# A two-layer decoder trunk on one core: the attention stage in another order, with compression in four additions and o split straight from its sums

## What is computed

```python
def compress_blocks(tok, pos, w1, w2):          # 15 blocks of 32 tokens, 4 groups
    blocks = blocks + pos[:, None, :]
    return jax.nn.gelu(flat @ w1) @ w2
...
qg = h @ w_qg                                    # q, and 3 gates for each of 16 heads
s_c = q . k_cmp;  p_c = masked_softmax(s_c);  o_c = p_c . v_cmp
s_s = q . k_slc;  p_s = masked_softmax(s_s);  o_s = p_s . v_slc
s_w = q . k_win;  p_w = masked_softmax(s_w);  o_w = p_w . v_win
o = g0 * o_c + g1 * o_s + g2 * o_w
return o @ w_o
```

## Time and profile before

| | |
|---|---|
| median of 3 runs | 877.27 us (876.54 to 877.97) |
| the profiled execution | 878.77 us, span 876.9 us |
| PE busy | 814.1 us (93%), 7626 instructions |
| DVE busy | 663.0 us (76%), 734 instructions |
| ACT busy | 424.1 us (48%) |
| POOL busy | 134.6 us (15%) |
| mean granted PE clock | 0.977 of 2.4 GHz |

### The profile page before, as it was taken

How to read it: one execution, slowest core, us unless ns; L and a number is a source line. 1 busy time by engine, 2 the same in 40 slices (tenths; PEclk the granted TensorE clock), 3 DMA queues, 4 the chain that set the end, 5 groups by cost and what they waited for, 6 DMA issues and landing times.

```text
span 876.9 us, 18026 instructions
## 1 busy us (share of the span) xinstructions
PE 814.1 (93%) x7626; PEld 705.2 (80%) x7626; DVE 663.0 (76%) x734; ACT 424.1 (48%) x610; POOL 134.6 (15%) x208
## 2 busy tenths in 40 slices
PE   2899999999899899999999899998888899999997
PEld 2699798788777599999997798965566899999975
DVE  5878988999876799999996665769854687555552
ACT  3366724565463744444444645148647454444441
POOL 8700004634623100000000222001110000000000
PEclk9899999999999999999999999969999999999999
DMA  9934254234340789999992687550005377555641
GB/s 349 341 105 161 85 168 151 103 100 146 123 148 28 286 312 371 379 377 375 377 351 67 214 262 212 169 221 1 1 2 191 112 279 237 191 191 192 192 144 49
DMA packets 71840, 170.20 MB, mean 194 GB/s; under 512 B 5433, under 2 KB 6737, under 8 KB 71761
## 3 DMA queue, kind: packets, MB, share of 16 engines
q1 hardware_dynamic: 68784, 160.75, 52.6%
q0 software_dynamic: 2416, 7.15, 3.0%
q10 hardware_dynamic: 560, 1.14, 0.4%
HBM read 166.42 MB, written 1.05 MB: 191 GB/s over the span
## 4 chain that ended last, share of the span: by engine, by line
PE 59%; DVE 30%; ACT 5%; issue 3%; DMA 3%; POOL 1%; SPq 0%; DVEq 0%; ACTq 0%; POOLq 0%
DVE wlo L1123 9%; DVE acc L1509 6%; PE ps L1896 5%; PE ps L1900 5%; PE ps L1898 5%; PE ps L1885 5%; PE ps L1887 5%; PE ps L1888 5%; PE ps L1791 2%; PE ps L1793 2%; PE ps L1794 2%; PE ps L2003 2%; ACT whi L662 2%; DMA raw<-in_ada_w_dram 2%; PE ps L1767 2%
## 5 line engine op out<-in xcount | busy, mean ns | idle before, releaser
L1123 DVE TENSOR_TENSOR wlo<-raw,whi 128x2048 fp32r<-128x2048 f32 (+1 forms) x98 | 217.2, 2216 | 59.2 <-ACT whi L662 57.0
L662 ACT ACTIVATE whi<-raw 128x2048 fp32r<-128x2048 f32 (+1 forms) x98 | 179.5, 1842 | 148.1 <-DMA raw<-in_mlp_down_dram 94.7
L1885 PE MATMUL ps<-ghi,whi 128*128 128x256 f32 x576 | 164.0, 285 | 7.9 <-ACT ghi L938 4.2
L1887 PE MATMUL ps<-glo,whi 128*128 128x256 f32 x576 | 163.7, 284 | 0.0
L1888 PE MATMUL ps<-ghi,wlo 128*128 128x256 f32 x576 | 163.7, 284 | 0.0
L1885 PEld LDWEIGHTS ps<-ghi,whi 128*128 128x128 f32 x576 | 111.2, 193 | 11.2 <-issue 7.5
L1887 PEld LDWEIGHTS ps<-glo,whi 128*128 128x128 f32 x576 | 111.2, 193 | 0.5
L1888 PEld LDWEIGHTS ps<-ghi,wlo 128*128 128x128 f32 x576 | 111.3, 193 | 0.0
L1896 PE MATMUL ps<-whi,hidhi 128*128 128x512 f32 x256 | 100.9, 394 | 2.2 <-DVE wlo L1123 2.0
L1898 PE MATMUL ps<-whi,hidlo 128*128 128x512 f32 x256 | 99.8, 390 | 0.0
L1900 PE MATMUL ps<-wlo,hidhi 128*128 128x512 f32 x256 | 99.6, 389 | 0.0
(11 more groups left out here) (380 smaller groups left out, 1618.9 us busy)
## 6 DMA issues: line engine op xcount, KB each, us to landing
raw<-in_mlp_up_dram SPq DMA_DIRECT2D x32, 1024.0 KB, 5.8
raw<-in_mlp_down_dram SPq DMA_DIRECT2D x32, 1024.0 KB, 5.2
raw<-in_ada_w_dram SPq DMA_DIRECT2D x24, 1024.0 KB, 5.6
late<-in_ada_w_dram SPq DMA_DIRECT2D x24, 1024.0 KB, 9.1
late<-in_kv_ada_w_dram SPq DMA_DIRECT2D x8, 1024.0 KB, 8.9
raw<-in_kv_w_dram SPq DMA_DIRECT2D x6, 1024.0 KB, 5.7
raw<-in_rw_k_dram SPq DMA_DIRECT2D x4, 1024.0 KB, 9.1
raw<-in_rw_r_dram SPq DMA_DIRECT2D x4, 1024.0 KB, 5.1
```

Source lines behind the costliest of these rows:

```text
L662: ins = sc.activation(whi[i][:, ks, :], raw[i][:, :].rearrange("p (k n) -> p k n", k=4)[:, ks, :], ACT.Copy)
L1123: ins = dv.tensor_tensor(wlo[i][:, ks, :], raw[i][:, :].rearrange("p (k n) -> p k n", k=4)[:, ks, :], whi[i][:, ks, :].bitcast(F32), ALU.s ...
L1885: mm(out_, whi[b][:, k, cols], hi[:, k0 + k, :], start=(first and k == 0 and m % 2 == 0), stop=False, skip_group_check=True)
L1887: mm(out_, whi[b][:, k, cols], lo[:, k0 + k, :], start=False, stop=False, skip_group_check=True)
```

## The change

Lines of the changed kernel are some 5 to 20 away from those before.

- DVE's 32 `xcmp` additions are 4, each over 8 positions at once (480 columns), with the position values as a second tensor. They stand before the low part of `q0 + 1`, and the compression is PE's first step, ahead of q.
- q is written as four single steps (`query(i)`), with the gate products, turning and scores of the first units in between.
- The compressed branch is done for 8 heads at a time: `cmp_scores(h)`, `cmp_shifted(h)`, `cmp_exps(h)`, `cmp_probs(h)`, `cmp_turn(h)`, `cmp_turned(h)`. Each product of its scores repeats its 30 columns up to four times; the next one writes over the repeats.
- The maxima come negated from the reduction; the separate negation is gone.
- DVE multiplies the probabilities of all units; POOL of none.
- `oT` and its copies are gone: after `outputs(u)` ACT makes the high part of the unit's o from bank 7, and DVE the low part from bank 7 and the high part. `outputs(u)` waits for the low part of unit u - 1. The second half of the projection waits for all 16.
- The orders of PE, ACT and DVE over the stage are other ones.

```diff
-                    for p in range(8):
-                        a = 8 * h + p
-                        ins = dv.tensor_scalar(xcmp[:, i, a, 0:60].rearrange("q (g n) -> q g n", n=NCMP), src[:, p],
-                                               pt2[:, pos + a:pos + a + 1], None, ALU.add)
+                        ins = dv.tensor_tensor(
+                            xcmp[:, i, 8 * h:8 * h + 8, 0:60].rearrange("q a (g n) -> q a g n", n=NCMP), src,
+                            pt2[:, at_:at_ + 8].unsqueeze(2).unsqueeze(3).to_broadcast([P, 8, G, NCMP]), ALU.add)
...
-                st.do(dv.tensor_reduce(mx[:, u, :].rearrange("p (e b) -> p e b", e=2), src, axis=AX.X, op=ALU.max))
-                st.tell(dv.tensor_scalar(nm[:, u, :], mx[:, u, :], -1.0, None, ALU.mult), T["nm"])
+                st.tell(dv.tensor_reduce(nm[:, u, :].rearrange("p (e b) -> p e b", e=2), src, axis=AX.X, op=ALU.max, negate=True),
+                        T["nm"])
...
-                if tb == 0:
-                    st.tell(factors, T["cf"])
-                else:
...
+                keys = P * (tb + 1)
+                own = prob[u % 2][:, :, :, 0:keys].rearrange("p e b k -> p (e b) k")
+                st.tell(dv.tensor_tensor(own, own, cf[:, u, :].unsqueeze(2).to_broadcast([P, 4, keys]), ALU.mult), T["pr"])
...
+            def o_high(u):
+                act.wait_ge(n_o_ps, u + 1)
+                sc.activation(ohi[:, j, P * tb:P * tb + P], ps[:, 7, 0:P], ACT.Copy).then_inc(n_zhi, 1)
...
+            def o_low(u):
+                v.wait_ge(n_zhi, NCH + u + 1)
+                st.tell(dv.tensor_tensor(olo[:, j, cols], ps[:, 7, 0:P], ohi[:, j, cols].bitcast(F32), ALU.subtract), T["zlo"])
...
+            def cmp_scores(h):
+                pe.wait_ge(n_c, 1)
+                pe.wait_ge(n_gates, 1)
+                pe.wait_ge(n_qT, h + 1)
                 for tb in range(TB):
+                    for j in range(4 * h, 4 * h + 4):
+                        c0 = 240 * h + 2 * NCMP * (4 * tb + j - 4 * h)
+                        times = min(4, (512 - c0) // (2 * NCMP))
+                        ins = mm(ps[:, 7, c0:c0 + 2 * NCMP * times], qT[:, j, P * tb:P * tb + P],
+                                 kcmp[:, j // 2, :, 0:NCMP].unsqueeze(1).to_broadcast([P, times, 2, NCMP]), start=True, stop=True)
...
             def outputs(u):
-                pe.wait_ge(n_pcT, 1)
+                pe.wait_ge(n_pcT, 1 if j < 4 else 2)
                 if u:
-                    pe.wait_ge(n_o, u)
+                    pe.wait_ge(n_zlo, NCH + u)
+                else:
+                    pe.wait_ge(n_scx, 2)
```

More of the change, by code:

```diff
@@ L329, in hybrid_kernel @@
         n_sc_ps, n_scx, n_sce, n_pc = (sem(n) for n in ("cmp_scores", "cmp_shifted", "cmp_exp", "cmp_probs"))
[L330 to L332 removed]
+        n_pr = sem("probs_scaled")
+        n_s_ps, n_nm, n_e, n_pT_ps, n_pT, n_pcT, n_o_ps = (sem(n) for n in (
+            "scores", "score_max", "exps", "probs_turned", "probs_copied", "cmp_probs_copied", "o_psum"))
         H_AT = {1: 2, 2: 6, 3: 8, 4: 12}
@@ new lines, in cmp_blocks @@
+            def cmp_blocks():
+                v.wait_ge(n_stk, 16 * 8)
+                for i, pos in enumerate((POSK, POSV)):
+                    for h in range(2):
+                        src = stk[:, i, :, :].rearrange("q g (n s) -> q s g n", s=16)[:, 0:16:2, :, h:h + NCMP]
+                        at_ = pos + 8 * h
+                        ins = dv.tensor_tensor(
+                            xcmp[:, i, 8 * h:8 * h + 8, 0:60].rearrange("q a (g n) -> q a g n", n=NCMP), src,
+                            pt2[:, at_:at_ + 8].unsqueeze(2).unsqueeze(3).to_broadcast([P, 8, G, NCMP]), ALU.add)
+                        st.tell(ins, T["xcmp"]) if i and h else st.do(ins)
@@ new lines, in gates_copied, with inner_copied @@
+            def gates_copied():
+                v.wait_ge(n_gt_ps, 1)
+                for b in range(TB):
+                    ins = dv.tensor_copy(gates[:, b, :, :].rearrange("p h i -> p (h i)"), ps[:, 7, P * b:P * b + 48])
+                    st.tell(ins, T["gates"]) if b else st.do(ins)
+            def inner_copied():
+                v.wait_ge(n_hc_ps, 1)
+                st.do(dv.tensor_copy(both(hc), ps[0:60, 2, 0:2 * P]))
+                st.do(dv.tensor_tensor(both(hx), both(hc), both(hc), ALU.mult))
+                st.do(dv.tensor_scalar(both(hx), both(hx), 0.044715, 1.0, ALU.mult, ALU.add))
+                st.tell(dv.tensor_tensor(both(hx), both(hx), both(hc), ALU.mult), T["hx"])
@@ L2311, in _, with gate_products, query @@
-            ins.then_inc(n_hc_ps, 1)
-            q_half(1)
+            def gate_products():
+                pe.wait_ge(n_wg, 16)
+                for k in range(KC):
+                    ins = mm(ps[0:48, 7, 0:S], wg[:, k, :], hfull[:, k, :], start=(k == 0), stop=(k == KC - 1))
+                ins.then_inc(n_g_ps, 1)
+            def query(i):
+                n, kh = i // 2, i % 2
+                if kh == 0:
+                    if n:
+                        pe.wait_ge(n_kv, 2)
+                        pe.wait_ge(n_vt, 2)
+                    else:
+                        pe.wait_ge(n_kc, 1)
+                parts_ready(q0 + i)
+                features(q0 + i, 0, [ps[:, 4 * n + m // 2, (m % 2) * S:(m % 2) * S + S] for m in range(4)],
+                         qhi, qlo, 4 * kh, kh == 0).then_inc(s_ws, 1)
@@ new lines, in gates_turn, with compress_inner @@
+            def gates_turn():
+                pe.wait_ge(n_gF, 1)
+                for b in range(TB):
+                    ins = tr(ps[:, 7, P * b:P * b + 48], gateF[:, P * b:P * b + P], ident[0:48, 0:48])
+                ins.then_inc(n_gt_ps, 1)
+            def compress_inner():
+                pe.wait_ge(n_xcmp, 1)
+                pe.wait_ge(n_w1, 16 * 5)
+                pe.wait_ge(n_kv, 1)
+                pe.wait_ge(n_vt, 1)
+                for i in range(2):
+                    for p in range(16):
+                        ins = mm(ps[0:60, 2, P * i:P * i + P], xcmp[:, i, p, 0:60], w1[i][:, p, :], start=(p == 0),
+                                 stop=(p == 15))
+                ins.then_inc(n_hc_ps, 1)
```

237 lines of the change are left out of this document (90 added, 147 removed).

## The result

| | before | changed |
|---|---|---|
| median of 4 runs | 876.90 us (874.63 to 877.97) | 868.44 us (866.71 to 869.46) |
| profiled execution / its span | 878.77 / 876.9 us | 867.99 / 866.2 us |
| mean granted clock of PE | 0.977 | 0.987 |
| last product of keys and values to first of the output projection | 537.75 to 649.72 = 112.0 us | 539.77 to 638.50 = 98.7 us |

The ratio is 0.9905 [0.9879, 0.9931]: 8.5 us faster, forecast 866.3. The last line of the table is the stage that the diff touches. It is 13.2 us shorter, the span 10.7. The rest is outside the diff: the profiled execution reaches the stage 2.0 us later than the one before did, through code that is the same, and behind it 0.5 is lost. Over the fourteen profiled executions of this document the stage starts between 537.4 and 540.5 us, so 2.0 is scatter between executions.

A forecast was written before the change was run, and what follows sets the result against it. No engine full in the loop: PE, DVE and ACT wait in turn; the opening has waits and a half-speed PE clock. 14.0 - 0.4 - 0.6 - 2.0 = 11.0 us off 878.8 gives 867.8, less 1.5 is 866.3; range 863.2 to 871.5 (84%).

The forecast's parts named there:

- The walk: Hand layout of every unit through the three engines' written orders, with each wait kept: output projection 14.0 us earlier.
- Front, 10.6 us: PE's stretch from the key/value projections to scores(4): scores(4) starts at 583.5 instead of 594.15, 10.6 us earlier.
- xcmp at 0.69 each: DVE's four additions before the compression: 0.69 us each, 2.8 in all, where 32 took 9.9 with gaps.
- the test that the prediction set: Prediction counts as wrong if PE waits over 1 us for xcmp.
- Loop, 52.2 us: Loop over the attention units, from scores(4) to the output projection: 52.2 us instead of 55.6.
- Hand-overs, 2.0 us off: Some 25 hand-overs between engines on the path, at 0.05 to 0.1 us each, cost 2.0 us.
- Last low parts, 0.4; wo pieces, 0.6: Before the output projection: two last low weight parts lose 0.4 us; first wo piece may land 0.6 after ACT wants it.
- 1.5 us from profiled to median: Median of the runs shown taken as 1.5 us below the profiled execution, turning 867.8 into 866.3.
- 6.5 + 1.5 for the clock: PE at half clock in the kernel before: 6.5 us more from 578 to 591, some 1.5 from 629 to 632.
- ACT as the loop's bound: Rival: ACT gets 3.6 us more in the loop and bounds it; gain 6.0, total 871.3 us; chance 12%.
- A clock that falls again in the stage: Rival: PE's clock falls for as long as from 578 to 591, costing 5 us, total 871.3; chance 8%.
- The slower rival, bank 7 with two readers: Rival: outputs wait for ACT and DVE to read bank 7, 1.7 us per unit, total 892 us; chance 4%.

The follow-up runs named there:

- the run with the source without a step: Changed kernel with the 4 xcmp additions reading 480 neighbouring columns of another tile instead of every sixteenth column: 864.89 us, ratio 0.9843.
- the control: The changed kernel run again with no edit: 866.46 us, ratio 0.9862 to the kernel before; stage 98.7 us.
- the three groups: Three groups of runs, each on a chip of its own; the kernel before had medians of 877.99, 879.31 and 878.68 us.
- order of the front (a mixture, see above): Changed kernel with the old order of gate products, q, compression and first scores, including a 3.40 us wait neither kernel has: 874.70 us, ratio 0.9956.
- low parts behind the loop: Changed kernel with the low part of the output projection's third weight piece made inside the loop again: 869.08 us, ratio 0.9903.
- the kernel with the pause filled: Kernel before, with two unused products between scores(0) and the compressed values, where PE had waited 1.9 us: 876.60 us, ratio 0.9976.

## Why the prediction was right, and where it was not

The sum stood at 867.8 for a profiled execution and the one taken was 867.99. That is nearer than its terms were. The walk had 14.0 us and 3.0 of losses were taken off it, of which only 0.24 can be seen. The stage gave 13.2, and 2.0 of late arrival and 0.5 behind it, which were in no term, filled the place of the 3.0. The mechanism was right; that the total came out to 0.2 is luck.

- **Front, 10.6 us.** Measured 9.98 within the stage. Cover, order and clock came as laid out: compressed values under q's pieces, no wait for hcTv, clock 1.00 in all of 560 to 585, halves of 1.94 and 1.89. The compressed turn, behind the queries' last piece, stood at 581.45; the walk's 578.7 is 581.9 with the 2.0 of late arrival and the 1.2 that xcmp made.
- **xcmp at 0.69 each.** This step failed, by the test that the prediction set: PE waited 1.59. The row taken for it, the reduction of 480 elements, reads without a step. The four took 4.04 in place of 2.8, 1.01 each with their gaps, and PE started 1.2 later than laid out (541.36, against 538.1 and 2.0 of late arrival); the run with the source without a step shows that the step in the source is the whole difference. The Trainium skill (VectorE: DVE Perf Modes, Mode 2×_2P) spoke of the second tensor as the cost. The trace agrees with it in that two fp32 tensors don't get two elements a cycle: from 512 to 1024 elements the scaling, with two fp32 operands, grows by 532 ns, 1.04 ns an element, which is one element a cycle at the 0.96 GHz of that page. The 328 ns of the step come on top of that.
- **Loop, 52.2 us.** Measured 52.3. From scores(4) on to (6), (8), (10), (12) and (14) the walk had 7.6, 7.6, 8.7, 5.4 and 8.9 us; measured 7.8, 7.8, 8.3, 5.5 and 8.6. So each step came out within 0.5, and the loop's near sum doesn't rest on large errors that cancel. outputs(5) and (13) did wait for the low part of o, by 0.50 and 0.96 (forecast 0.95 and 0.7). A wait of 1.25 at turn(4) for DVE's scaling lies where the prediction shows no details. ACT's small high parts took 282 ns, not 370, so ACT got 2.2 us more and not 3.6.
- **Hand-overs, 2.0 us off.** They cost nothing that can be seen: the walk had its loop to 0.1. The 2.0 was taken off without a row of its own.
- **Last low parts, 0.4; wo pieces, 0.6.** 0.24 of wait was seen for the low part, and none for a wo piece.
- **1.5 us from profiled to median.** This failed. The sum was made against an execution 1.9 over the median of the four runs, while the changed kernel's profiled one lay 0.45 under its median. The stage's 13.2 us is measured against the same dear execution; the medians say 8.5, and 12.9 in the control's group.
- **What the clock gave.** Over the 31, 17 and 11 runs of the kernel before in the three groups, span and mean clock go together (correlation -0.82, -0.77, -0.81; the clock from 0.973 to 0.989). A line through each puts that kernel at 870.8 to 873.8 us for the changed kernel's clock of 0.989, its median spans being 876.2 to 877.5. So some 3 to 5 us of the gain is clock, and 6 to 9 is left at equal clock, against the control's 864.7. It is an estimate: the line runs to its end there. The prediction had counted 6.5 + 1.5 for the clock. Its reading missed a third stretch, at scores(4) behind the wait of 2.51 there (busy time of PE, PEld, DVE, ACT, POOL, then clock, DMA share, GB/s):

```profile
594.00:599.00 5.00, 4.85 (x22) 2.32 (x22) 4.33 (x11) 5.00 (x13) 1.04 (x1) 0.66 0.00 0
```

That is 1.7 us more. All of it gone, as in the two executions of the changed kernel, is some 10 us of PE's time out of this stage; not all of that is on the path.
- **Rivals.** ACT as the loop's bound did not come: 44.9 of 52 busy, as said, but PE's waits fell on both others, 4.9 us on DVE and 3.0 on ACT. A clock that falls again in the stage did not come in the two profiled executions of the changed kernel, while in each of the other twelve kernels' profiles it fell at least once, also where the edit comes only after the fall. So the changed kernel is near to it, and whether 8% was too little two profiles don't tell. The slower rival, bank 7 with two readers, falls clearly: 2.3 us in sum where 0.73 a unit was its point, and with one reader again the time rose and did not fall, if for the large portions' sake.

What each part is worth when it is undone alone, in us (by the ratios: above the control, of 878):

| part undone | stage | by the ratios |
|---|---|---|
| order of the front (a mixture, see above) | 7.9 | 8.3 |
| additions | 8.0 | 8.0 |
| o from its sums | 5.1 | 6.9 |
| negation | 5.1 | 3.8 |
| scaling on DVE | 2.2 | 2.5 |
| low parts behind the loop | 5.2 | 3.6 |

The first two are not to be added: each needs the other. The last three lie within the 3.8 us by which the changed kernel itself differed between two groups of runs, and two of their stages are those of the slowest of six executions. They come to far more than 13.2, and in each of these stages 3 to 10 us passed at 1.2 GHz that the control has not. That the same falls are counted several times is likely, but no run with several parts undone shows it.

**Open.** Why the clock fell behind one pause of 1.90 us within 2 us, behind another of 1.72 some 6 us later, behind 1.94 and 1.97 in front of the compression, not at all behind pauses of 1.57 to 1.82 there in five executions, and once with no pause, no run settles. Nor was an order tried that hides the last 1.59: contiguous sources would need the stacked inputs written in another layout.

## What to carry to other kernels

Find what makes the costliest pause of the bounding engine and put its independent work there, but price the producer of the first thing in the new order: here the time of a few additions decided whether the reordering gave anything. For an operation that no row shows, take a row with the same access pattern, not only the same count. Where the clock of TensorE moves with its pauses, compare medians with their clocks, not two profiled executions.

## What the runs showed of the hardware

- A fp32 addition over 480 elements took 658 ns with a contiguous source and 986 ns with a source step of 64 bytes. Eight small ones of 60 elements with the same step took 280 each.
- A maximum that negates cost the same as the plain one: 1224 and 692 ns.
- The clock's fall can come with PE fully busy: in the kernel with the pause filled, PE waited for nothing from 554 to 581 and ran at 0.50 from 581 to 587.
- Low stretches in this stage, where the executions differ most: some 20 us in the profiled execution before, 14 with the additions alone, 7 with the negation alone (an edit that touches neither pause), 0 in both of the changed kernel.
- One pause of 2.76 us on PE in the loop was followed by 7 us at 1.2 GHz; the stage grew by 5.2.
- 16 passes of 30 columns took 1.87 us at the high clock, 16 of up to 120 columns 1.94 and 1.89.
